# A fused transformer-style block in float32: the first modulation computed by halves of its columns and summed straight into columns, with the first weight unit interleaved between its parts

## Chip, cores and metric

The kernel runs on one core of one Trainium2 chip. The metric is the device time of one execution in microseconds (us); lower is better. The kernel is given as one Python program that writes the instruction stream of each engine: TensorE (PE), VectorE (DVE), ScalarE (ACT), GpSimd (POOL) and SyncE (SP, which issues all DMAs). The engines meet through semaphores alone, and each works off its own list in order.

## What is computed

One layer of a residual block on x of 1 x 1024 x 1024 and a conditioning vector c of 1024. What matters here is its beginning:

```python
c_act = jax.nn.silu(c)
mod = c_act @ w_ada[l] + b_ada[l]                       # 1024 -> 6 x 1024
shift1, scale1, gate1, shift2, scale2, gate2 = jnp.split(mod, N_MOD, axis=-1)
h = _rmsnorm(x, norm_mix_g[l]) * (1.0 + scale1) + shift1
z = h @ w_in[l]                                         # 1024 -> 6144
...
```

After it come the convolution, the gated recurrence, the spatial gating, the branch projections, the output projection, a second modulated norm, the up projection, a convolution and the down projection, and a last norm. All of that is the same in both kernels.

## The kernel before

**Layout.** Activations are kept transposed: channels on the 128 partitions in 8 tiles (KT = 8, KH = 4), tokens along the free dimension (S = 1024 in two halves of 512). A float32 product is made of three products of rounded operands: each operand is split into a high part (made by ACT) and a low part (the difference, made by DVE). The weight's halves are `wop` (four slots, filled by `hi(n)` on ACT, L1109, and `lo(n)` on DVE, L1648); the normed input's halves are `yq` (made by `norm_high` on ACT, L1164, and `norm_low` on DVE, L1715).

**Units.** The input projection runs as units, one after the other on PE. The first, G0, is plain: `first_gates` (L854) takes 12 matmuls for each of the 8 channel tiles, in two groups of 6, and needs `norm_low(k)` of a tile before its 12. From the second, G1, on a unit is done in seven block products (`product7`, L764, 12 matmuls each) in the order b11, t1, t2, b22, t3, b21, t4. t1 to t4 are sums and differences of normed blocks. DVE makes them (`u_sum`, L1719), ACT rounds them (`u_high`, L1179 and L1183) and DVE makes the low parts (`u_low`, L1729 and L1733). POOL makes four sums of weight blocks for each such unit (L617 to L628).

**The beginning.** SP loads x, the parameter rows, the columns of `w_ada` for scale1 (`ada_s`) and shift1 (`ada_h`), 4 MB each, and then weights. PE transposes x (L689), DVE and ACT copy it out of PSUM, and ACT sums squares (L1132). ACT's last steps of this stretch are the copies of the parameter columns (L1124), which PE awaits before it starts the modulation, a table load and the square root (L1151); DVE makes the diagonal matrix of inverse norms (L1697), and PE spreads it over the partitions (L728, the result stays in `ps3`).

**The modulation.** c_act lies as 8 columns, `cact`. For scale1 and shift1 in turn, PE makes rows: `modulation_row` (L708) has a column of `cact` as its weight, 128x1, and streams a row tile of `w_ada` of 1024 columns. This is done for four of the eight tiles; DVE sums the other four, scaled, into an accumulator (`mod_pieces`, L1685 and L1687), and PE adds that up over the partitions (`add_row`, L712). The result is a row of 1024 numbers on one partition. ACT and DVE copy half of it each out of PSUM (L1155, L1703), and PE turns it into columns with eight matmuls whose weight is a 1x128 piece (`row_to_columns`, L717). DVE adds the bias. In float32 each of these matmuls shows as two records in the profile.

**The order of the rest.** `normed(k)` (L1710, DVE) multiplies x by the inverse norm, `scaled(k)` (L1160, ACT) by 1 + scale. When shift is there as columns (`shift_ready`), ACT starts `norm_high(0)`, DVE follows with `norm_low(0)`, and PE starts G0. The place of each piece of work on DVE and ACT is written out by hand (DVE L1736 to L1776, ACT L1186 to L1206). Nothing plans it.

Of the kernel before, what the change touches and what calls it, by code (L numbers as in the profile page):

```python
# [11 lines left out]
P = 128  # L12
# [5 lines left out]
def build(nc, a, out):  # L18
# [54 lines left out]
    with ExitStack() as ctx:  # L73
# [41 lines left out]
        ada_s = place("ada_s", [KT, D], F32, "H")  # L115
        ada_h = place("ada_h", [KT, D], F32, "Y", 2 * QUAD)
# [5 lines left out]
        scale_row = place("scale_row", [D], F32, "WSP", 2 * TILE)  # L122
        shift_row = place("shift_row", [D], F32, "WSP", 3 * TILE)
        scale_acc = place("scale_acc", [D], F32, "WSP", 1 * TILE)
        shift_acc = place("shift_acc", [D], F32, "T", 1 * TILE)
# [105 lines left out]
        def blocks(t):  # L231
# [6 lines left out]
        scale_landed = [sem(f"scale_landed{i}") for i in range(KT // 2)]  # L238
        shift_landed = [sem(f"shift_landed{i}") for i in range(KT // 2)]
# [3 lines left out]
        acc_ready, row_sum, row_ready, row_cols, s1_ready, shift_ready = (  # L243
            sem(x) for x in ("acc_ready", "row_sum", "row_ready", "row_cols", "s1_ready", "shift_ready"))
        xhat_ready, tn_ready, norm_hi, norm_lo, spilled = sem("xhat_ready"), sem("tn_ready"), sem("norm_hi"), sem("norm_lo"), sem("spilled")
# [159 lines left out]
        def _(sp):  # L405
# [11 lines left out]
            def load_modulation(dst, part, landed):  # L417
                for i in range(KT // 2):
                    k = slice(ADA_CHUNKS[i], ADA_CHUNKS[i + 1])
                    sp.dma_start(dst[:, k, :], w_ada[:, k, part * D:(part + 1) * D]).then_inc(landed[i], 16)  # L420
# [237 lines left out]
        def _(pe):  # L658
# [47 lines left out]
            def modulation_row(psum, w, k, first):  # L706
                for h in range(2):
                    nc.tensor.matmul(psum[0:1, h, :], cact[:, k:k + 1], w[:, k, H[h]], start=first, stop=False)  # L708

            def add_row(psum, acc):  # L710
                for h in range(2):
                    last = nc.tensor.matmul(psum[0:1, h, :], ones[:, 0:1], acc[:, H[h]], start=False, stop=True)  # L712
                return last

            def row_to_columns(psum, row):
                for j in range(KT):
                    last = nc.tensor.matmul(psum[:, j:j + 1], row[0:1, j * P:(j + 1) * P], ones[0:1, 0:1], start=True, stop=True)  # L717
                return last
# [3 lines left out]
            for k in SCALE_ROWS:  # L722
                pe.wait_ge(scale_landed[CHUNK_OF[k]], 16)
                modulation_row(ps[1], ada_s, k, k == SCALE_ROWS[0])
                if k == SCALE_ROWS[1]:
                    pe.wait_ge(x_diag, 1)
                    for h in range(2):
                        norm = nc.tensor.matmul(ps[3][:, h, :], ones[:, :],  # L728
                                                diag0[:, HB * h:HB * h + HB, :].rearrange("p b t -> p (b t)"),
                                                start=True, stop=True)  # L730
                    norm.then_inc(x_rbc, 1)
            pe.wait_ge(acc_ready, 1)
            add_row(ps[1], scale_acc).then_inc(row_sum, 1)
            pe.wait_ge(row_ready, 2)
            row_to_columns(ps[0][:, 0, :], scale_row).then_inc(row_cols, 1)
            for k in SHIFT_ROWS:
                pe.wait_ge(shift_landed[CHUNK_OF[k]], 16)
                modulation_row(ps[2], ada_h, k, k == SHIFT_ROWS[0])
            pe.wait_ge(acc_ready, 2)
            add_row(ps[2], shift_acc).then_inc(row_sum, 1)  # L740
            pe.wait_ge(row_ready, 4)
            row_to_columns(ps[0][:, 1, :], shift_row).then_inc(row_cols, 1)
# [102 lines left out]
            def first_gates():  # L845
                for k in range(KT):
                    pe.wait_ge(norm_lo, k + 1)
                    for s, psum in enumerate(BANKS[0]):
                        n = 2 * (k // KH) + s
                        if k % KH == 0:  # L850
                            ready(n)
                        for w, x in PRODUCTS:
                            for h in range(2):
                                done = nc.tensor.matmul(psum[:, h, :], wop[n][:, w, k % KH, :], normed(k, x, h),  # L854
                                                        start=(k == 0 and w == 0 and x == 0), stop=(k == KT - 1 and w == 1))
                        if k % KH == KH - 1:
                            done.then_inc(used, 1)
# [243 lines left out]
        def _(act):  # L1101
# [25 lines left out]
            for c in range(4):  # L1127
                act.wait_ge(x_landed[c], 16)
                for i in (2 * c, 2 * c + 1):
                    if i:  # L1130
                        act.wait_ge(x_squared, i)
                    nc.scalar.activation(sq0[:, :], xtok[:, i, :], ACT.Square, accum_out=ss[:, i:i + 1])\  # L1132
                        .then_inc(x_squared, 1)
                for i in (2 * c, 2 * c + 1):
# [4 lines left out]
                if c == 1:  # L1139
# [5 lines left out]
                    nc.scalar.activation(lt[:, 1, :], lt[:, 0, :], ACT.Exp, scale=-1.0).then_inc(lam_e, 1)  # L1145
            act.wait_ge(param_T, 2)
            for t in range(1, len(ROWS)):
                param_copy(t)
            act.wait_ge(eps_made, 1)
            act.wait_ge(x_squared, NB)  # L1150
            nc.scalar.activation(rs[:, :], ss[:, :], ACT.Sqrt, bias=epsc, scale=1.0 / D).then_inc(x_root, 1)  # L1151

            def row_half(row, psum, n):
                act.wait_ge(row_sum, n)
                nc.scalar.activation(row[0:1, H[0]], psum[0:1, 0, :], ACT.Copy).then_inc(row_ready, 1)  # L1155

            def scaled(k):
                act.wait_ge(s1_ready, 1)
                act.wait_ge(xhat_ready, k + 1)
                nc.scalar.activation(tn[:, k, :], tn[:, k, :], ACT.Identity, scale=s1[:, k:k + 1]).then_inc(tn_ready, 1)  # L1160
# [25 lines left out]
            row_half(scale_row, ps[1], 1)  # L1186
            for k in range(KH):
                scaled(k)
            hi(0)
            scaled(KH)  # L1190
            row_half(shift_row, ps[2], 2)
            hi(1)
            scaled(KH + 1)
# [5 lines left out]
            scaled(KT - 2)  # L1199
            scaled(KT - 1)  # L1200
# [432 lines left out]
        def _(dve):  # L1633
# [29 lines left out]
            def modulation(dst, part, g):  # L1663
                return V.scalar_tensor_tensor(dst[:, :], mod[:, part * KT:(part + 1) * KT], 1.0, C(g, 0, KT),
                                              ALU.add, ALU.mult)
# [4 lines left out]
            V.memset(eps_t[:, :], EPS).then_inc(eps_made, 1)  # L1670
            for i in range(NB):
# [9 lines left out]
            def mod_pieces(acc, w, pieces, k0, landed, done):  # L1681
                for k in pieces:
                    dve.wait_ge(landed[CHUNK_OF[k]], 16)
                    if k == k0:
                        ins = V.tensor_scalar(acc[:, :], w[:, k, :], cact[:, k:k + 1], None, ALU.mult)  # L1685
                    else:
                        ins = V.scalar_tensor_tensor(acc[:, :], w[:, k, :], cact[:, k:k + 1], acc[:, :], ALU.mult, ALU.add)  # L1687
                    if done is not None and k == pieces[-1]:
                        ins.then_inc(done, 1)
                    else:  # L1690
                        step(ins)

            dve.wait_ge(cact_ready, 1)
            mod_pieces(scale_acc, ada_s, (0,), 0, scale_landed, None)
# [4 lines left out]
            mod_pieces(scale_acc, ada_s, (4, 5, 7), 0, scale_landed, acc_ready)  # L1699

            def row_half(row, psum, n):
                dve.wait_ge(row_sum, n)
                V.tensor_copy(row[0:1, H[1]], psum[0:1, 1, :]).then_inc(row_ready, 1)  # L1703

            def normed(k):
# [4 lines left out]
                V.tensor_tensor(tn[:, k, :], x0T[:, k, :], flat(ps[3]), ALU.mult).then_inc(xhat_ready, 1)  # L1710
# [25 lines left out]

            normed(0)
            row_half(scale_row, ps[1], 1)
            normed(1)
            dve.wait_ge(row_cols, 1)  # L1740
            step(V.tensor_tensor(mod[:, KT:2 * KT], ps[0][:, 0, 0:KT], C("b_ada", KT, KT), ALU.add))
            modulation(s1, 1, "norm_mix_g").then_inc(s1_ready, 1)
            normed(2)
            mod_pieces(shift_acc, ada_h, (0, 1), 0, shift_landed, None)
            normed(3)
            mod_pieces(shift_acc, ada_h, (4, 5), 0, shift_landed, acc_ready)
            normed(4)
            lo(0)
            row_half(shift_row, ps[2], 2)
            normed(5)  # L1750
            lo(1)
            dve.wait_ge(row_cols, 2)
            step(V.tensor_tensor(mod[:, 0:KT], ps[0][:, 1, 0:KT], C("b_ada", 0, KT), ALU.add))
# [591 lines left out]
```

## Time and profile before

| | us |
|---|---|
| median of 3 runs (lowest, highest) | 1575.05 (1574.47, 1578.14) |
| the profiled execution | 1574.12 |
| its span, first to last instruction | 1572.1 |
| PE busy | 1536.0 (98%) |
| DVE busy | 1185.2 (75%) |
| ACT busy | 805.2 (51%) |
| POOL busy | 386.2 (25%) |

The span is 2.0 us shorter than the profiled execution's own time. PE busy counts pipelined matmuls by modelled ends, so it can't be read as PE at its peak. The change touches what happens up to about 85 us. The lists of the engines behind that are the same in both kernels.

### The profile page before, as it was taken

How to read it: one execution, taken by the hardware profiler on the slowest of the kernel's cores; microseconds unless marked ns; L12 is line 12 of the kernel's file. 1: busy time of each engine (PE TensorE's matmuls, PEld its weight loads, DVE VectorE, ACT ScalarE, POOL GpSimd, SP SyncE). 2: the span in 40 equal slices, each digit the busy share in tenths (PEclk: the TensorE clock that was granted, in tenths of full speed). 3: DMA queues.
4: the chain of work that ended last, by engine and by line, in shares of the span. 5: the costliest groups of instructions: out<-in, count | busy, mean ns of one | idle time of the engine just before them, and what ended most of it. 6: DMA issues, size and time to landing. Idle time of an engine off the chain costs nothing.

```text
span 1572.1 us, 19429 instructions
## 1 busy us (share of the span) xinstructions
PE 1536.0 (98%) x6860; PEld 1254.4 (80%) x6860; DVE 1185.2 (75%) x1418; ACT 805.2 (51%) x1194; POOL 386.2 (25%) x292
## 2 busy tenths in 40 slices
PE   7999999999999999999998989999999999999998
PEld 3677777888888888888886878888888888888886
DVE  5968889845565685466337999999999987788885
ACT  4648888745545461112123655555555554444446
POOL 0232344332122200000000233333333331233324
PEclk9999999999999999999999999999999999999999
DMA  9331223222322347667210134444444446677722
GB/s 364 133 107 57 82 67 101 65 83 81 101 77 92 107 142 234 180 214 241 94 54 28 49 133 158 151 153 147 148 148 148 150 139 224 208 246 253 253 68 107
DMA packets 197791, 219.55 MB, mean 140 GB/s; under 512 B 8928, under 2 KB 155712, under 8 KB 197056
## 3 DMA queue, kind: packets, MB, share of 16 engines
q1 hardware_dynamic: 197696, 218.32, 41.9%
q8 instruction: 55, 0.90, 0.2%
q14 instruction: 40, 0.33, 0.1%
HBM read 160.61 MB, written 57.67 MB: 139 GB/s over the span
## 4 chain that ended last, share of the span: by engine, by line
PE 82%; DVE 12%; issue 3%; ACT 2%; DMA 0%; POOLq 0%; POOL 0%; ACTq 0%; DVEq 0%
PE ps L764 57%; PE ps L835 15%; DVE wop L1648 3%; DVE xc L1805 2%; PE ps L854 2%; PE ps L958 1%; PE ps L1048 1%; PE ps L708 1%; PE ps L1030 1%; DVE ps L1661 1%; PE ps L901 1%; DVE ti L1823 1%; DVE hidw L2125 1%; ACT wop L1109 1%; DVE m L1828 1%
## 5 line engine op out<-in xcount | busy, mean ns | idle before, releaser
L1648 DVE TENSOR_TENSOR wop<-raw,wop 128x512 fp32r<-128x512 f32 (+1 forms) x523 | 378.8, 731 | 177.2 <-ACT wop L1109 174.9
L1109 ACT ACTIVATE wop<-raw 128x512 fp32r<-128x512 f32 (+1 forms) x523 | 296.5, 569 | 391.1 <-PE ps L764 187.8
L764 PE MATMUL ps<-yq,wop 128*128 128x512 f32 x1716 | 415.9, 392 | 5.9 <-DVE yq L2084 4.7
L764 PEld LDWEIGHTS ps<-yq,wop 128*128 128x128 f32 x1716 | 323.5, 189 | 76.4 <-issue 4.0
L617 POOL TENSOR_TENSOR raw<-raw,raw 128x512 f32<-128x512 f32 (+1 forms) x65 | 96.3, 1482 | 889.2 <-DVE wop L1648 648.6
L764 PE MATMUL ps<-dq,wop 128*128 128x512 f32 x840 | 190.6, 389 | 0.0
L764 PEld LDWEIGHTS ps<-dq,wop 128*128 128x128 f32 x840 | 157.7, 188 | 32.7
L764 PE MATMUL ps<-t4q,wop 128*128 128x512 f32 x540 | 132.9, 396 | 6.8 <-DVE ps L1661 6.8
L764 PE MATMUL ps<-t3q,wop 128*128 128x512 f32 x540 | 130.7, 391 | 2.0 <-issue 1.7
L764 PE MATMUL ps<-t2q,wop 128*128 128x512 f32 x540 | 130.5, 391 | 0.5 <-ACT snap_p L1119 0.5
L764 PE MATMUL ps<-t1q,wop 128*128 128x512 f32 x540 | 130.6, 391 | 0.0
L764 PEld LDWEIGHTS ps<-t4q,wop 128*128 128x128 f32 x540 | 101.6, 190 | 32.3 <-DVE ps L1661 11.4
L1119 ACT ACTIVATE snap_p<-ps 128x512 f32<-128x512 f32 x130 | 77.6, 597 | 93.1 <-PE ps L764 93.0
L2125 DVE SCALAR_TENSOR_TENSOR hidw<-ps,pc,hidw 128x1023 f32<-128x1023 f32 x96 | 122.4, 1276 | 0.9
L1661 DVE TENSOR_TENSOR ps<-ps,snap_p 128x512 f32<-128x512 f32 x130 | 90.2, 694 | 43.1 <-PE ps L764 42.1
L764 PEld LDWEIGHTS ps<-t2q,wop 128*128 128x128 f32 x540 | 101.1, 188 | 22.7 <-ACT snap_p L1119 1.2
L764 PEld LDWEIGHTS ps<-t3q,wop 128*128 128x128 f32 x540 | 100.6, 188 | 23.3 <-issue 2.1
L764 PEld LDWEIGHTS ps<-t1q,wop 128*128 128x128 f32 x540 | 100.8, 188 | 20.6
L628 POOL TENSOR_TENSOR raw<-raw,raw 128x512 f32<-128x512 f32 (+1 forms) x65 | 75.4, 1160 | 89.2 <-DVE wop L1648 85.8
L624 POOL TENSOR_TENSOR raw<-raw,raw 128x512 f32<-128x512 f32 (+1 forms) x65 | 80.9, 1244 | 64.5 <-DVE wop L1648 60.5
L620 POOL TENSOR_TENSOR raw<-raw,raw 128x512 f32<-128x512 f32 (+1 forms) x65 | 90.2, 1387 | 9.3
L835 PE MATMUL ps<-ya_split,wop 128*128 128x512 f32 x384 | 87.8, 390 | 0.0
(235 smaller groups left out, 1929.0 us busy)
## 6 DMA issues: line engine op xcount, KB each, us to landing
dq<-hid_keep SPq DMA_DIRECT2D x35, 1024.0 KB, 7.1
raw<-in_w_in SPq DMA_DIRECT2D x96, 256.0 KB, 3.3
raw<-in_w_up SPq DMA_DIRECT2D x96, 256.0 KB, 3.3
hid_keep<-part_b SPq DMA_DIRECT2D x40, 512.0 KB, 3.0
ada_ring<-in_w_ada SPq DMA_DIRECT2D x32, 512.0 KB, 4.6
hid_keep<-part_t SPq DMA_DIRECT2D x20, 512.0 KB, 2.7
raw<-in_w_down SPq DMA_DIRECT2D x80, 128.0 KB, 2.4
gate_keep<-tg SPq DMA_DIRECT2D x16, 512.0 KB, 4.0
```

What stands on the lines that cost most here:

```text
L617: nc.gpsimd.tensor_tensor(s1, a21, a22, ALU.add).then_inc(s_made, 1)
L620: nc.gpsimd.tensor_tensor(a21, a11, a21, ALU.subtract).then_inc(s_made, 1)
L624: nc.gpsimd.tensor_tensor(a11, s1, a11, ALU.subtract).then_inc(s_made, 1)
L628: nc.gpsimd.tensor_tensor(s1, a12, a11, ALU.subtract).then_inc(s_made, 1)
L764: done = nc.tensor.matmul(bank, left[:, w, lk, :], right[:, x, rk, :], start=(first and w == 0 and x == 0), stop=(last and w == 1), skip_g ...
L835: done = nc.tensor.matmul(psum[:, h, :], wop[n % 4][:, w, k % KH, :], right(k, x, h), start=(k == 0 and w == 0 and x == 0), stop=(k == KT ...
L854: done = nc.tensor.matmul(psum[:, h, :], wop[n][:, w, k % KH, :], normed(k, x, h), start=(k == 0 and w == 0 and x == 0), stop=(k == KT - 1 ...
L1109: nc.scalar.activation(wop[n % 4][:, 0, 0:depth[n], :], raw[slot][:, 0:depth[n], :], ACT.Copy).then_inc(f_hi, 1)
L1119: nc.scalar.activation(dst[:, :], src, ACT.Copy).then_inc(snapped, 1)
L1648: V.tensor_tensor(wop[n % 4][:, 1, 0:kd, :], raw[slot_of[n][0]][:, 0:kd, :], wop[n % 4][:, 0, 0:kd, :].bitcast(F32), ALU.subtract).then_in ...
L1661: V.tensor_tensor(out_b, in_b, kept[:, :], ALU.add).then_inc(joined, 1)
L2125: tap = V.scalar_tensor_tensor(dst[:, d:S], src[:, 0:S - d], C("ffn_conv_w01" if k < 2 else "ffn_conv_w2", k % 2 * 2 * FT + f), dst[:, d:S ...
```

## The change

- `w_ada` is loaded in four parts of 512 columns, `ada_w[0..3]`: scale1 of the channel tiles 0 to 3, shift1 of the same, scale1 of tiles 4 to 7, shift1 of the same. Each is 2 MB, in one DMA of 6 row tiles and one of 2. The weights of G0 are loaded between them: A11 and A21 ahead of part 2, A12 and A22 ahead of part 3.
- For each part PE makes columns at once: the weight is a 128x128 block of `w_ada`, and the moving operand is one column of `cact`. Four matmuls for each row tile, all summed in PSUM (`modulation_columns`). A matmul of the identity with zeros opens the sum (`modulation_begin`), and four matmuls with the accumulator of DVE as their weight close it (`modulation_end`). PE takes 4, 4, 5 and 5 row tiles of the parts, DVE the other 4, 4, 3 and 3, now 512 wide.
- Rows, their copies out of PSUM and `row_to_columns` are gone, and so is `scaled(k)` on ACT: `normed(k)` on DVE now multiplies by scale and inverse norm in one instruction.
- G0 starts when parts 0 and 1 are done. Part 2 is begun just ahead of its tile 0 and ended ahead of tile 1; part 3 is begun ahead of tile 3 and ended ahead of tile 4. `shift_ready` now counts two halves.
- ACT takes the square root ahead of the last copy of x, and loads its table after the fourth square. It copies the last parameter columns behind both.
- DVE's and ACT's lists up to G1 are written in a new order.

```diff
-        ADA_CHUNKS = (0, 3, 6, 7, 8)
-        CHUNK_OF = (0, 0, 0, 1, 1, 1, 2, 3)
-        SCALE_ROWS, SHIFT_ROWS = (1, 2, 3, 6), (2, 3, 6, 7)
+        ADA_SPLIT = 6
+        SCALE_PARTS, SHIFT_PARTS = (0, 2), (1, 3)
+        PE_ROWS = ((0, 1, 2, 6), (0, 1, 2, 6), (0, 1, 2, 3, 6), (0, 1, 2, 3, 6))
...
-            load_modulation(ada_s, 1, scale_landed)
-            load_modulation(ada_h, 0, shift_landed)
-            weights(0)
+            load_modulation(0)
+            load_modulation(1)
+            weights(0, 0, 2)
+            load_modulation(2)
+            weights(0, 2, 4)
+            load_modulation(3)
             weights(1, 0, 2)
...
+            def modulation_columns(p, rows):
+                for k in rows:
+                    pe.wait_ge(ada_landed[p][k // ADA_SPLIT], 16)
+                    for j in range(KH):
+                        nc.tensor.matmul(ps[0][:, p % 2, P + KH * p + j:P + KH * p + j + 1], ada_w[p][:, k, j * P:(j + 1) * P],
+                                         cact[:, k:k + 1], start=False, stop=False, skip_group_check=True)
+
+            def modulation_begin(p):
+                nc.tensor.matmul(ps[0][:, p % 2, P + KH * p:P + KH * p + KH], ident[:, :], dsh[:, :], start=True, stop=False,
+                                 skip_group_check=True)
+                modulation_columns(p, PE_ROWS[p][:-1])
+
+            def modulation_end(p):
+                modulation_columns(p, PE_ROWS[p][-1:])
+                pe.wait_ge(acc_ready, p + 1)
+                for j in range(KH):
+                    last = nc.tensor.matmul(ps[0][:, p % 2, P + KH * p + j:P + KH * p + j + 1], ada_sum1[p % 2][:, j * P:(j + 1) * P],
+                                            ones[:, 0:1], start=False, stop=True, skip_group_check=True)
+                last.then_inc(cols_ready, 1)
...
+            modulation_begin(0)
+            pe.wait_ge(x_diag, 1)
+            for h in range(2):
+                norm = nc.tensor.matmul(ps[3][:, h, :], ones[:, :],
+                                        diag0[:, HB * h:HB * h + HB, :].rearrange("p b t -> p (b t)"),
+                                        start=True, stop=True)
+            norm.then_inc(x_rbc, 1)
+            modulation_end(0)
+            modulation_begin(1)
+            modulation_end(1)
...
             def first_gates():
+                pe.wait_ge(shift_ready, 1)
+                modulation_begin(2)
                 for k in range(KT):
+                    if k == 1:
+                        modulation_end(2)
+                    if k == KH - 1:
+                        modulation_begin(3)
+                    if k == KH:
+                        modulation_end(3)
                     pe.wait_ge(norm_lo, k + 1)
...
-                V.tensor_tensor(tn[:, k, :], x0T[:, k, :], flat(ps[3]), ALU.mult).then_inc(xhat_ready, 1)
+                V.scalar_tensor_tensor(tn[:, k, :], x0T[:, k, :], s1[:, k:k + 1], flat(ps[3]), ALU.mult, ALU.mult).then_inc(tn_ready, 1)
```

The order of PE around the start of G0, before. `ps2` and `ps1` are the outputs of G0, `ps0` holds the columns of the modulation.

```order
L708 MATMUL ps2<-ada_h_73,cact_182 1x512 [waits shift_landed3]
L708 MATMUL ps2<-ada_h_73,cact_182 1x512
L712 MATMUL ps2<-shift_acc_82,ones_177 1x512 [waits acc_ready]
L712 MATMUL ps2<-shift_acc_82,ones_177 1x512
L717 MATMUL ps0<-ones_177,shift_row_80 128x1 [waits row_ready]
L717 MATMUL ps0<-ones_177,shift_row_80 128x1 x7
L854 MATMUL ps2<-yq_49,wop0_63 128x512 [waits f_lo,norm_lo]
L854 MATMUL ps2<-yq_49,wop0_63 128x512 x5
L854 MATMUL ps1<-yq_49,wop1_64 128x512 [waits f_lo]
L854 MATMUL ps1<-yq_49,wop1_64 128x512 x5
```

And after, from the end of tile 2 of G0 to its tile 4:

```order
L857 MATMUL ps1<-yq_49,wop1_64 128x512 x6
L713 MATMUL ps0<-dsh_196,ident_176 128x4
L709 MATMUL ps0<-cact_182,ada_w3_75 128x1 [waits ada_landed3_0]
L709 MATMUL ps0<-cact_182,ada_w3_75 128x1 x3
...
L857 MATMUL ps2<-yq_49,wop0_63 128x512 [waits norm_lo]
L857 MATMUL ps2<-yq_49,wop0_63 128x512 x5
L857 MATMUL ps1<-yq_49,wop1_64 128x512 x6
L709 MATMUL ps0<-cact_182,ada_w3_75 128x1 [waits ada_landed3_1]
L709 MATMUL ps0<-cact_182,ada_w3_75 128x1 x3
L721 MATMUL ps0<-ones_177,ada_sum1_1_82 128x1 [waits acc_ready]
L721 MATMUL ps0<-ones_177,ada_sum1_1_82 128x1 x3
L857 MATMUL ps2<-yq_49,wop2_65 128x512 [waits f_lo,norm_lo]
```

The shift of the upper tiles, which was complete ahead of G0, is now complete between its tiles 3 and 4.

DVE at the same place, before, from the low parts of tiles 2 and 3 on:

```order
L1715 SCALAR_TENSOR_TENSOR yq<-tn,mod,yq 128x2x512 x2
L1719 TENSOR_TENSOR t1w<-tn 128x2048
L1648 TENSOR_TENSOR wop_65<-raw_59,wop_65 128x512
L1648 TENSOR_TENSOR wop_66<-raw_60,wop_66 128x512
L1715 SCALAR_TENSOR_TENSOR yq<-tn,mod,yq 128x2x512 x4
L1648 TENSOR_TENSOR wop_63<-raw_61,wop_63 128x512
L1719 TENSOR_TENSOR t2w<-tn,t1w 128x2048
L1729 TENSOR_TENSOR t1q<-t1w,t1q 128x2048
L1719 TENSOR_TENSOR tn<-tn,t2w 128x4x512
L1648 TENSOR_TENSOR wop_64<-raw_59,wop_64 128x512
```

And after, from the wait for the last columns (`cols_ready`) on:

```order
L1687 TENSOR_TENSOR mod_178<-ps0,pc_175 128x4 [waits cols_ready]
L1757 TENSOR_TENSOR dsh1_195<-mod_178 128x4 [waits shift_ready]
L1710 SCALAR_TENSOR_TENSOR yq_49<-tn_77,mod_178,yq_49 128x2x512 [waits norm_hi]
L1705 SCALAR_TENSOR_TENSOR tn_77<-x0T_76,s1_179,ps3 128x1024
L1710 SCALAR_TENSOR_TENSOR yq_49<-tn_77,mod_178,yq_49 128x2x512 [waits norm_hi]
L1714 TENSOR_TENSOR t1w_54<-tn_77 128x2048
L1710 SCALAR_TENSOR_TENSOR yq_49<-tn_77,mod_178,yq_49 128x2x512 [waits norm_hi]
L1714 TENSOR_TENSOR t2w_55<-tn_77,t1w_54 128x2048 [waits u_made]
L1710 SCALAR_TENSOR_TENSOR yq_49<-tn_77,mod_178,yq_49 128x2x512 [waits norm_hi]
L1637 TENSOR_TENSOR wop0_63<-raw4_61,wop0_63 128x512 [waits f_hi]
L1637 TENSOR_TENSOR wop1_64<-raw2_59,wop1_64 128x512 [waits f_hi]
```

The low parts of tiles 4 to 7, one `normed` and both sums of the t chain now stand behind a wait for PE's columns.

## Rows read from the trace of the kernel before

**Rows 1.** Busy time by stage: stretch, length, busy time and instructions, PEclk, DMA share, GB/s

```profile
17.60:19.94 2.34, 0.00 (x0) 0.00 (x1) 1.43 (x2) 2.32 (x7) 0.00 (x0) 1.00 1.04 415
19.94:51.14 31.20, 26.64 (x77) 8.10 (x77) 21.46 (x26) 12.95 (x15) 0.00 (x0) 0.85 1.05 392
51.14:75.06 23.92, 23.92 (x97) 19.62 (x98) 23.82 (x16) 15.80 (x19) 7.03 (x3) 0.92 0.07 21
```

**Rows 2.** PE in order of time up to G0: start, length, what, idle before

```profile
19.94 5.29 PE L708 MATMUL ps<-ada_s,cact 128*1 128x512 f32 x8 [2.34 <-ACT pc L1124]
25.16 1.98 PE L728 MATMUL ps<-diag,ones 128*128 128x512 f32 x4
33.16 2.23 PE L717 MATMUL ps<-ones,scale_row 1*128 1x1 f32 x16 [0.77 <-DVE scale_row L1703]
46.19 1.94 PE L717 MATMUL ps<-ones,shift_row 1*128 1x1 f32 x16 [0.77 <-DVE shift_row L1703]
51.14 1.22 PE L854 MATMUL ps<-yq,wop 128*128 128x512 f32 x2 [3.01 <-DVE yq L1715]
```

**Rows 3.** DVE in order of time: first modulation piece, then from the first low part on

```profile
19.41 0.75 DVE L1685 TENSOR_SCALAR scale_acc<-ada_s,cact 128x1024 f32<-128x1024 f32 x1 [0.91 <-DMA ada_s<-in_w_ada]
...
49.80 1.28 DVE L1715 SCALAR_TENSOR_TENSOR yq<-tn,mod,yq 128x1024 fp32r<-128x1024 f32 x1 [1.27 <-ACT yq L1164]
51.00 1.21 DVE L1710 TENSOR_TENSOR tn<-x0T,ps 128x1024 f32<-128x1024 f32 x1
56.85 2.28 DVE L1719 TENSOR_TENSOR t1w<-tn 128x2048 f32<-128x2048 f32 x1
60.26 6.93 DVE L1715 SCALAR_TENSOR_TENSOR yq<-tn,mod,yq 128x1024 fp32r<-128x1024 f32 x4
70.10 3.20 DVE L1729 TENSOR_TENSOR t1q<-t1w,t1q 128x2048 fp32r<-128x2048 f32 x1
76.03 3.77 DVE L1733 SCALAR_TENSOR_TENSOR t2q<-t2w,mod,t2q 128x512 fp32r<-128x512 f32 x4
79.72 0.68 DVE L1648 TENSOR_TENSOR wop<-raw,wop 128x512 fp32r<-128x512 f32 x1
80.32 2.28 DVE L1719 TENSOR_TENSOR tn<-tn 128x2048 f32<-128x2048 f32 x1
85.23 2.74 DVE L1733 SCALAR_TENSOR_TENSOR t3q<-tn,dsh,t3q 128x512 fp32r<-128x512 f32 x4 [1.43 <-ACT t3q L1183]
```

**Rows 4.** PE in units G1 and R0: product t3, and two products in a row

```profile
88.07 3.00 PE L764 MATMUL ps<-t3q,wop 128*128 128x512 f32 x12 [1.72 <-issue]
...
99.34 2.88 PE L764 MATMUL ps<-t1q,wop 128*128 128x512 f32 x12
102.06 2.88 PE L764 MATMUL ps<-t2q,wop 128*128 128x512 f32 x12
```

**Rows 5.** ACT in order of time, from the fourth square to the root

```profile
18.50 1.00 ACT L1137 ACTIVATE x0T<-ps 128x1024 f32<-128x1024 f32 x1
19.41 0.48 ACT L1124 ACTIVATE pc<-ps 128x96 f32<-128x96 f32 x3
19.91 1.28 ACT L1151 ACT_TABLE_LOAD   x1
21.20 0.30 ACT L1151 ACTIVATE rs<-ss,eps_t 128x8 f32<-128x8 f32 x1
```

**Rows 6.** PE at 623 us: column sums with 128x128 weights, and what follows

```profile
623.81 1.84 PE L703 MATMUL ps<-ones,ada_acc 128*128 128x1 f32 x16
625.51 3.25 PE L835 MATMUL ps<-ya_split,wop 128*128 128x512 f32 x13
```

**Rows 7.** PE by stretch: length, PE busy and matmuls, PEclk, DMA share, GB/s

```profile
34.65:38.07 3.42, 3.42 (x9) 0.50 1.16 304
48.30:55.14 6.84, 4.00 (x9) 0.50 0.44 144
85.80:89.20 3.40, 1.68 (x8) 1.00 0.54 189
```

More of the change, by code:

```diff
@@ L121, in build @@
         diag0 = place("diag0", [NB, P], F32, "T", 3 * TILE)
[L122 to L125, printed above, removed]
+        ada_sum1 = [place(f"ada_sum1_{i}", [HALF], F32, "T", 1 * TILE + i * 4 * HALF) for i in range(2)]
         xc_split = place("xc_split", [2, S], F32R, "X")
@@ L415, in load_x, with load_modulation @@
                 sp.dma_start(xtok[:, 2 * i:2 * i + 2, :], x_tok[:, 2 * i:2 * i + 2, :]).then_inc(x_landed[i], 16)
[L417 to L420, printed above, removed]
+            def load_modulation(p):
+                c0 = (D if p in SCALE_PARTS else 0) + p // 2 * HALF
+                for i, k in enumerate((slice(0, ADA_SPLIT), slice(ADA_SPLIT, KT))):
+                    sp.dma_start(ada_w[p][:, k, :], w_ada[:, k, c0:c0 + HALF]).then_inc(ada_landed[p][i], 16)
             def weights(pos, start=0, stop=4):
@@ L704, in column_sums @@
                 return last
[L706 to L718, printed above, removed]
+            def modulation_columns(p, rows):
[4 more added lines that the diff above has]
+                                         cact[:, k:k + 1], start=False, stop=False, skip_group_check=True)
@@ L720, in _ @@
             for e in range(2):
                 pe.wait_ge(xT_copied[e], COPIER.count(e))
[L722 to L731, printed above, removed]
@@ L1133, in _ @@
                         .then_inc(x_squared, 1)
+                if c == 3:
+                    act.wait_ge(x_squared, NB)
+                    nc.scalar.activation(rs[:, :], ss[:, :], ACT.Sqrt, bias=epsc, scale=1.0 / D).then_inc(x_root, 1)
                 for i in (2 * c, 2 * c + 1):
@@ L1148, in _ @@
                 param_copy(t)
[L1149 to L1160, printed above, removed]
             def norm_high(k):
@@ L1198, in _ @@
             hi(3)
[L1199 to L1200 removed]
+            act.wait_ge(shift_ready, 2)
             for k in range(KH, KT):
@@ L1680, in _, with mod_pieces, mod_columns, scale_columns @@
                     V.tensor_tensor(lt[:, 0, :], lt[:, 2, :], lam, ALU.max).then_inc(lam_e, 1)
[L1681 to L1685, printed above, removed]
-                    else:
-                        ins = V.scalar_tensor_tensor(acc[:, :], w[:, k, :], cact[:, k:k + 1], acc[:, :], ALU.mult, ALU.add)
-                    if done is not None and k == pieces[-1]:
-                        ins.then_inc(done, 1)
+            def mod_pieces(p, rows):
+                acc, mine = ada_sum1[p % 2], [k for k in range(KT) if k not in PE_ROWS[p]]
+                for k in rows:
+                    dve.wait_ge(ada_landed[p][k // ADA_SPLIT], 16)
+                    if k == mine[0]:
+                        ins = V.tensor_scalar(acc[:, :], ada_w[p][:, k, :], cact[:, k:k + 1], None, ALU.mult)
+                    else:
+                        ins = V.scalar_tensor_tensor(acc[:, :], ada_w[p][:, k, :], cact[:, k:k + 1], acc[:, :], ALU.mult, ALU.add)
+                    if k == mine[-1]:
+                        ins.then_inc(acc_ready, 1)
                     else:
                         step(ins)
+            def mod_columns(p):
+                dve.wait_ge(cols_ready, p + 1)
+                c0 = (KT if p in SCALE_PARTS else 0) + p // 2 * KH
+                return V.tensor_tensor(mod[:, c0:c0 + KH], ps[0][:, p % 2, P + KH * p:P + KH * p + KH], C("b_ada", c0, KH), ALU.add)
+            def scale_columns(p):
+                step(mod_columns(p))
+                step(modulation(s1, 1, "norm_mix_g", p // 2 * KH, p // 2 * KH + KH))
             dve.wait_ge(cact_ready, 1)
-            mod_pieces(scale_acc, ada_s, (0,), 0, scale_landed, None)
             dve.wait_ge(x_root, 1)
```

93 lines of the change are left out of this document (38 added, 55 removed).

## The prediction, made before any run of the changed kernel

> **What bounds the kernel now.** I read the busy time by stage first. From the start of the modulation at 19.94 to G0's first matmul at 51.14 PE is busy for 26.6 of 31.2 us, DVE for only 21.5 of them; from there to G0's end at 75.06 PE is without a gap and DVE is busy for 23.8 of 23.9 [rows 1]. So PE carries the first stretch, and both are full in the second. PE's list in order of time shows what the first stretch is made of: row matmuls, the spreading of the norms, eight column matmuls each for scale and shift, two waits of 0.77 for the copies of a row out of PSUM, and 3.01 us of waiting for the first low part [rows 2].
>
> Then I followed G1, since it shows who is late behind G0. Its product t3 starts at 88.07 after 1.72 us of idling that is put down to issue [rows 4]. DVE's list names the cause. The last sum, which t3 is made from, runs from 80.32 to 82.60, ACT rounds it, and DVE's low part of t3 ends at 87.97 [rows 3]. **So the end of this beginning is set by DVE**, which works almost without a pause from 49.80 to 82.60. PE could be at t3 1.7 us sooner and gain nothing. Behind t3 the lists are equal and all of it shifts with t3's start. The question is therefore: does t3 start ahead of 88.07?
>
> **The change, part by part.**
>
> *ACT's head.* PE awaits the last parameter copies, which end at 19.89. Now the table load (1.28), an added small root and the real root (0.30 each) stand ahead of them [rows 5]: 1.9 us, with the steps between 2.1. PE starts the modulation at about 22.0 instead of 19.94. DVE has the root a microsecond earlier, which nobody needs.
>
> *PE's new work.* A float32 matmul gives two records. Parts 0 and 1 have 2 + 5 x 8 = 42 records each, parts 2 and 3 have 2 + 6 x 8 = 50, together 184. The nearest row is the column sum at 623 us, the same 128x128 weights and one column: 16 records from 623.81 to 625.51, so 0.106 each, 19.5 us in all [rows 6]. The other end is the present column matmul with 1x128 weights, 2.23 / 16 = 0.139 [rows 2]; I take 0.106 for the shape. Before, 48 row and sum records and 32 column records made up most of 26.6 us, so PE's work is hardly less, and 100 of the 184 records now stand behind the start of G0's stretch. To them come the norms, 1.9 [rows 2], and G0's tiles 0 to 3 at 2.72 each, the pace of two products in a row [rows 4], 10.9.
>
> *The clock.* PE ran its first row matmuls partly at 1.2 GHz (mean grant 0.85 in the stretch [rows 1]). After a longer idle time now I count the 26 records ahead of the norms at half speed, +2.8.
>
> *Waits.* 0.3 for the half shift ahead of part 2, 0.5 for DVE's accumulator of part 2. Columns of part 3 are complete at 22.0 + 19.5 + 1.9 + 10.9 + 2.8 + 0.8 = **57.9**.
>
> *DVE behind it.* Its list has everything up to `wop3` done by about 53, so it waits there for some 5 us. Then comes the bias, ACT's first high part, and the low part of tile 4 starts 1.5 later, at 59.4 (before, the same hop put tile 0's at 49.80 [rows 3]). From there to the end of the last sum: four low parts and one `normed` at 1.20 (spacing of two starts), three sums and the low part of t1 at 2.2, three weight low parts at 0.6, t2's low parts 2.7, the last sum 2.3: 21.6. POOL's sums slow DVE: t1's low part took 3.20 against 2.28 for a sum of that size, t2's 3.77 against 2.74 for t3's [rows 3]; +1.9. End at 59.4 + 23.5 = **82.9, against 82.60 before**. The 1.8 us that POOL cost in the four low parts (6.93 against 5.1) are saved, since POOL's first two sums now fall into DVE's wait; this is inside the sum. The 88.07 becomes 88.4.
>
> The page GPSIMD Engine Reference of the Trainium skill, in its table of properties, says that POOL shares its SBUF interfaces with VectorE and contends with instructions of two SBUF inputs. By that rule one more sum would be slowed by about 0.9 us, to 1576.3; the trace shows such a sum beside POOL unslowed, and the measurement decides.
>
> *Costs of nothing.* G0 itself ends at about 73 instead of 75.06: tile 7's low part is ready at 69.9, then 2.7. It is swallowed: product t2 waits for its low parts until 80.7, and t3 waits for the chain above. ACT loses eight `scaled` (9 us), but is not late anywhere. `normed` with its third operand is taken at 1.20 like a low part. The loads: the first 1.5 MB of `w_ada` had landed by 19.41 [rows 3]; at 0.39 MB per us [rows 1] part 1 is complete at 26, needed at 31, part 3 at 39, needed at 50. Loads in pieces of half the length could be a third slower and still be hidden; if this cover were gone, each late microsecond of part 1 or 3 would count fully.
>
> Sum: +0.3. The profiled execution, 1574.12, becomes 1574.4. That run lies 0.9 below the median, so the median of 1575.05 becomes **1575.4**. A difference under 0.3% (4.7 us) can't be told from none here.
>
> **The rivals.**
>
> *Slower: the clock stays at 1.2 GHz over the one-column matmuls.* For: the clock was granted at 0.50 from 34.65, behind 1.5 us of column matmuls and a gap of 0.77, and from 48.30, again right behind them [rows 2, 7]. Within wide products an idle time of 1.72 us left it at 1.00 [rows 7]. So narrow work seems to hold the clock badly, and now it is all that PE does from 22 to 39 but for two matmul pairs. Against: those weights had one row, they came with a gap, and the clock came back at 38.07 over a stretch that began with them. It decides at about 28 to 31 us: if the grant is still 0.50 there, 58 records of parts 0 and 1 and 34 of part 2 cost 0.106 more each (9.8), the norms 1.9, and the first wide matmuls, as from 51.14 on, about 1.5. That is 13, and up to 17 if part 3 loses the clock again. All of it lies ahead of 57.9, so it counts in full: about 1588, between 1583 and 1592. If it comes back after the norms, it costs 2, and that belongs to the forecast.
>
> The Trainium skill (TensorE: Matmul & The Clock Gate, section What's actually happening) has the clock set by how busy PE has been. By that rule unbroken narrow work is busy work and the forecast stands at 1575.4; it does not say whether matmuls of one column count, and only the rows above bear on that.
>
> *Slower by price:* a record costs 0.139. 158 of them at full clock: +5.2, 1580.6.
>
> *Faster:* DVE's wait for part 3 is the slack. If the clock is full from the start (-2.8), POOL costs DVE nothing behind 59.4 (-1.9) and the waits of 0.8 are gone, t3 starts 5.5 sooner, 1569.9. Each alone stays within 0.3%. That the change does what it says isn't in doubt: both orders show it.
>
> **How the numbers follow.** Forecast with its neighbours (1571 to 1579): 0.45. Clock: 0.32. Price or another late piece: 0.06. Faster: 0.17. So same 0.45, slower 0.38, faster 0.17. The range leaves out a part of the faster case and the tail of the clock's: 1569.5 to 1589.
>
> **What would show it.** Right: part 3's columns at 57 to 59 us, DVE idle 4 to 6 us ahead of them, G0 done near 73, t3 of G1 at 88 to 89 after a wait of over 2 us, records of one column 0.10 to 0.11 apart, grant at 1.00 by 28 to 31. Wrong: a grant of 0.50 past 31; one-column records apart by more than 0.12 at full clock; a t3 that does not wait for DVE; or any wait for a load.

## The result, and the profile after

The changed kernel takes **1589.49 us** (median of 4 runs, 1587.38 to 1591.42), the kernel before in the same comparison 1574.76 (4 runs, 1574.07 to 1578.14). The ratio is 1.01, with a 95% interval of 1.0088 to 1.0113: slower by 14.7 us. The forecast was 1575.4 with a range up to 1589.0. The rival "the clock stays at 1.2 GHz" gave about 1588, between 1583 and 1592. The profiled spans, 1589.1 against 1572.1, lie 17.0 apart, more than the medians: the change's profile is of one of its longer executions.

PE in order of time, the part that answers to [rows 2] (start, length, what, idle before):

```profile
22.37 0.59 PE L713 MATMUL ps<-dsh,ident 128*128 128x4 f32 x2 [4.54 <-ACT pc L1127]
22.82 5.26 PE L709 MATMUL ps<-cact,ada_w 128*128 128x1 f32 x24
27.94 3.76 PE L731 MATMUL ps<-diag,ones 128*128 128x512 f32 x4
...
33.62 5.44 PE L709 MATMUL ps<-cact,ada_w 128*128 128x1 f32 x32
...
41.47 6.96 PE L709 MATMUL ps<-cact,ada_w 128*128 128x1 f32 x32
48.30 4.89 PE L857 MATMUL ps<-yq,wop 128*128 128x512 f32 x12
53.02 0.95 PE L709 MATMUL ps<-cact,ada_w 128*128 128x1 f32 x8
53.83 1.03 PE L721 MATMUL ps<-ones,ada_sum 128*128 128x1 f32 x8
54.72 5.69 PE L857 MATMUL ps<-yq,wop 128*128 128x512 f32 x24
60.39 4.95 PE L709 MATMUL ps<-cact,ada_w 128*128 128x1 f32 x32
65.20 4.97 PE L857 MATMUL ps<-yq,wop 128*128 128x512 f32 x12
```

Equal work stands here at two prices. Eight column records at 53.02 are 0.10 apart, the eight behind them 0.11; the 32 at 41.47 are 0.21 apart. A tile of G0 (x12) takes 4.89 at 48.30, while two tiles (x24) take 5.69 at 54.72. The stretches of the same profile say which clock was granted (length, PE, PEld, DVE, ACT, POOL, PEclk, DMA share, GB/s), and answer to [rows 1, 7]:

```profile
22.00:28.00 6.00, 5.63 (x27) 5.63 (x27) 5.15 (x8) 0.80 (x4) 0.00 (x0) 0.50 1.09 357
...
31.95:35.35 3.40, 3.40 (x32) 3.40 (x32) 1.64 (x4) 0.00 (x0) 0.00 (x0) 0.99 1.12 339
35.35:48.00 12.65, 12.40 (x59) 12.31 (x58) 8.98 (x11) 5.42 (x6) 0.00 (x0) 0.50 1.11 433
...
52.20:62.20 10.00, 10.00 (x63) 8.85 (x61) 7.10 (x10) 0.00 (x0) 0.58 (x1) 0.99 0.09 26
62.20:69.20 7.00, 7.00 (x28) 6.13 (x28) 0.00 (x0) 0.00 (x0) 2.34 (x2) 0.53 0.13 37
```

The clock came back at about 32 us, behind the norms, and was gone again from 35.35 on. At that moment PE stood in the middle of part 1's 32 records, without a pause before it. From 62.2 it fell once more, inside part 3's 32 records. PE is busy for 12.40 of 12.65 us at a grant of 0.50: being busy in this sense did not hold the clock.

DVE and PE behind part 3, which answer to [rows 3, 4]:

```profile
71.89 0.16 DVE L1687 TENSOR_TENSOR mod<-ps,pc 128x4 f32<-128x4 f32 x1 [9.75 <-PE ps L721]
73.26 1.28 DVE L1710 SCALAR_TENSOR_TENSOR yq<-tn,mod,yq 128x1024 fp32r<-128x1024 f32 x1 [1.02 <-ACT yq L1160]
...
87.05 2.29 DVE L1714 TENSOR_TENSOR tn<-tn,t2w 128x2048 f32<-128x2048 f32 x1
91.19 1.31 DVE L1637 TENSOR_TENSOR wop<-raw,wop 128x512 fp32r<-128x512 f32 x1 [1.84 <-ACT wop L1112]
```
```profile
102.82 3.00 PE L759 MATMUL ps<-t3q,wop 128*128 128x512 f32 x12 [1.72 <-issue]
```

DVE waits 9.75 us for the columns of part 3, which come at 71.89. Product t3 of G1 starts at 102.82 instead of 88.07, 14.75 later. Nothing absorbs it: at about 584 us the first matmuls of a group (L830) and at 1334 those of another (L1033) are still 14.7 and 14.6 us late. The other 2.4 us between the two spans arise behind 1340 us, where the lists are the same; no run isolates what they are. So 14.75 at t3 and 14.7 between the medians agree only roughly.

### The profile page after: what moved, and what is told of

Same layout as the page of the kernel before. It is cut to its first block, busy times and chain, and to the rows that moved or that the text cites. A ratio compares the mean times of both kernels' runs of the same rounds, so it can differ in the third digit from the quotient of the medians.

```text
span 1589.1 us, 19648 instructions
## 1 busy us (share of the span) xinstructions
PE 1548.6 (97%) x6972; PEld 1280.8 (81%) x6972; DVE 1181.9 (74%) x1426; ACT 795.1 (50%) x1185; POOL 387.7 (24%) x292
## 4 chain that ended last, share of the span: by engine, by line
PE 80%; DVE 12%; issue 3%; ACT 3%; POOL 1%; DMA 1%; POOLq 0%; ACTq 0%; DVEq 0%
PE ps L759 55%; PE ps L830 15%; DVE wop L1637 3%; DVE xc L1801 2%; PE ps L709 2%; PE ps L961 1%; PE ps L1051 1%; PE ps L1033 1%; DVE ps L1650 1%; PE ps L857 1%; PE ps L904 1%; DVE ti L1819 1%; DVE hidw L2121 1%; ACT wop L1112 1%; DVE m L1824 1%
## 5 line engine op out<-in xcount | busy, mean ns | idle before, releaser
L830 PE MATMUL ps<-yb_split,wop 128*128 128x512 f32 x384 | 87.8, 390 | 0.0
```

The costliest lines, as they stand in the source:

```text
L830: done = nc.tensor.matmul(psum[:, h, :], wop[n % 4][:, w, k % KH, :], right(k, x, h), start=(k == 0 and w == 0 and x == 0), stop=(k == KT ...
```

## Experiments

Each run compares with the kernel before on the same chip. The median of the kernel before was 1574.3 beside the first four (wide64, wide128, insert1, insert64), 1573.8 beside the next four (wide16, head64, early64, both64) and 1573.3 beside the last three.

**wide64: the same matmuls, but 64 equal columns wide.** The weights, the records and their order are those of the change. Only the moving operand is wider, the sums lie at other PSUM columns to make room, and DVE reads one column in 64.

```diff
-                        nc.tensor.matmul(ps[0][:, p % 2, P + KH * p + j:P + KH * p + j + 1], ada_w[p][:, k, j * P:(j + 1) * P],
-                                         cact[:, k:k + 1], start=False, stop=False, skip_group_check=True)
+                        nc.tensor.matmul(ps[0][:, p % 2, part_at(p) + WIDE * j:part_at(p) + WIDE * j + WIDE], ada_w[p][:, k, j * P:(j + 1) * P],
+                                         cact[:, k:k + 1].to_broadcast([P, WIDE]), start=False, stop=False, skip_group_check=True)
```

(The zero matmul of `modulation_begin` and the sum in `modulation_end` are widened in the same way.)

> The changed kernel, but every one-column matmul of the modulation now moves 64 equal columns (the same column of cact, or of ones, 64 times) and DVE reads one in 64 of the results; same weights, same order, same number of matmuls. Clock theory (one-column matmuls do not hold TensorE's clock, and the half clock is the whole loss): the grant returns to 1.00 before the norms, stays there through parts 1, 2 and 3, the columns of part 3 are complete at 57 to 60 us instead of 71.8, G1's t3 starts at 88 to 90 instead of 102.8, total 1574 to 1578. Price theory (the loss lies in the number of weight loads and their order on TensorE, whatever the clock): the wider operand cannot help, 1589 or more. Third (waiting on VectorE's list sets the time): under 2 us change, 1588 to 1590.

Measured: 1579.64 (5 runs, 1577.35 to 1580.99), ratio 1.0037 (1.0022 to 1.0051). By the medians 9.4 of 14.7 us are back. PE, DVE, then the stretches:

```profile
36.97 3.68 PE L714 MATMUL ps<-cact,ada_w 128*128 128x64 f32 x32
40.46 3.00 PE L862 MATMUL ps<-yq,wop 128*128 128x512 f32 x12
...
90.49 3.00 PE L764 MATMUL ps<-t3q,wop 128*128 128x512 f32 x12 [0.23 <-issue]
```
```profile
59.55 0.16 DVE L1692 TENSOR_TENSOR mod<-ps,pc 128x4 f32<-128x4 f32 x1 [5.69 <-PE ps L726]
```
```profile
22.00:28.00 6.00, 6.00 (x25) 4.68 (x25) 4.02 (x6) 0.42 (x1) 0.00 (x0) 0.57 1.09 361
...
36.00:52.00 16.00, 15.65 (x97) 13.81 (x97) 15.58 (x20) 5.42 (x6) 0.00 (x0) 1.00 1.04 402
```

The 32 records of part 2 take 3.68 instead of 6.96, although they stream 64 times as much. Part 3's columns come at 59.55 instead of 71.89. The clock theory had the direction and most of the size, but claimed too much: the grant was 0.50 until about 28.5 us, over the norms too, t3 came at 90.49 instead of 88 to 90, and the median is 1579.64 instead of 1574 to 1578. So the half clock is not the whole loss. The profile is of the fastest of the five executions.

**wide128 and wide16: how wide it has to be.** `WIDE` is 128 or 16, with the sums placed in PSUM to fit.

> The same with 128 equal columns. Clock theory: clock as with 64, but 128 columns no longer hide behind the weight load, so up to 0.05 us more for each of 184 records (+0 to +9 us against 64 columns). Price theory: 1589 plus those 0 to 9 us.

> The change with each one-column modulation matmul moving 16 equal columns instead (DVE reads one in 16). Between 1 column (clock at 0.50 for 10.3 + 17 us in this stretch, 1589.5) and 64 columns (0.50 only until 28.5, 1579.6). Theory (it is the idle array, few moved columns per weight load, that lets the clock fall): with 16 columns the clock still falls somewhere in parts 0 to 2, since the array is busy for a quarter as long as with 64; time between 1582 and 1589. Rival (any more than a single column will do, one column being a special form of matmul): the clock stays as in wide64, time 1578 to 1581.

Measured, one run each: 1578.73 with 128 columns, 1586.41 with 16. With 128 the clock is at 1.00 from 28 us to 60 and 32 records take 3.73, so 128 columns cost no more than 64, against the expectation's up to 0.05 for each record. With 16 it fell as in the change, for part 2 too, but the 32 records of part 3, from 59.26 to 62.80, kept 1.00:

```profile
34.00:50.00 16.00, 15.74 (x68) 15.12 (x68) 12.02 (x14) 5.41 (x6) 0.00 (x0) 0.50 1.06 408
...
60.00:64.00 4.00, 4.00 (x32) 3.83 (x32) 0.93 (x2) 0.00 (x0) 2.91 (x2) 1.00 0.23 66
```

So the loss is no property of the single column alone: 16 lose the clock too, though not in every part; 64 and 128, once the clock was up, did not lose it in any part.

**insert1 and insert64: the same in isolation.** The kernel before, with 48 unneeded matmuls (96 records) in the fourth ZV unit, where the clock is at 1.00 and PE has no idle time. One column in the first, 64 in the second:

```diff
+                if SEQ[pos] == ("ZV", 3) and w == 4:
+                    pe.wait_ge(*outputs_read(pos - 1, 0))
+                    for j in range(48):
+                        nc.tensor.matmul(past[0][:, 0, 0:1], ident[:, :], ones[:, 0:1], start=True, stop=True)
```

> The kernel before, with 48 unneeded float32 matmuls (128x128 weights, ONE column moved; 96 records) put in one row into the densest stretch, in the fourth ZV unit near 350 us. Nothing waits for them and TensorE has no idle time there. Clock theory: the grant falls to 0.50 inside the row though TensorE never pauses, so the row takes 14 to 20 us instead of the 10.2 that 96 records of 0.106 take, and the first wide matmuls behind it run at half speed; total +15 to +21. Rival (the clock fell only because of pauses and the late start of the beginning): the grant stays at 1.00, total +10 to +11.

> The same inserted row, but each matmul moves 64 columns. Clock theory: the grant stays at 1.00, row 10 to 12 us, total +10 to +12. If the number of weight loads without much streaming is what lowers the clock, it falls here too: +15 to +21.

Measured, one run each: 1594.02 and 1586.14. PE and stretches of the one with one column:

```profile
347.66 17.21 PE L891 MATMUL ps<-ones,ident 128*128 128x1 f32 x96
364.73 4.66 PE L764 MATMUL ps<-t3q,wop 128*128 128x512 f32 x12
```
```profile
345.00:351.00 6.00, 6.00 (x44) 5.53 (x42) 2.72 (x3) 1.75 (x3) 3.18 (x3) 1.00 0.15 44
...
352.00:358.00 6.00, 6.00 (x30) 6.00 (x29) 0.00 (x0) 0.00 (x0) 0.00 (x0) 0.50 0.00 0
```

And of the one with 64:

```profile
349.15 10.82 PE L891 MATMUL ps<-ones,ident 128*128 128x64 f32 x96
359.78 3.01 PE L764 MATMUL ps<-t3q,wop 128*128 128x512 f32 x12
```
```profile
352.00:358.00 6.00, 6.00 (x56) 6.00 (x56) 0.00 (x0) 0.00 (x0) 0.10 (x1) 1.00 0.01 3
```

PE never pauses in either. With one column it runs 30 records in 6 us at 0.50, with 64 it runs 56 at 1.00. The price is 17.21 against 10.82 for the row, and the product behind it takes 4.66 instead of 3.01. Both hit their expectations: +19.7 and +11.8 against the kernel before. Hardly a load is under way when the clock falls in insert1 (DMA share 0.01 from 350 to 351 us, 0.06 in the next), and insert64 has more (0.29 from 351 to 352) and keeps 1.00. This shows it apart from the rest of the change: the clock falls by the kind of work, with no gap to blame.

**head64, early64, both64: what is left of the loss.** On the 64-column version, ACT's head is put back as before (`head64`), part 3 is begun ahead of G0's tile 1 and ended ahead of tile 2 (`early64`), or both.

```diff
-                if c == 3:
-                    act.wait_ge(x_squared, NB)
-                    nc.scalar.activation(rs[:, :], ss[:, :], ACT.Sqrt, bias=epsc, scale=1.0 / D).then_inc(x_root, 1)
...
-                    act.wait_ge(eps_made, 1)
-                    nc.scalar.activation(sd[:, :], epsc, ACT.Sqrt)
...
             for t in range(1, len(ROWS)):
                 param_copy(t)
+            act.wait_ge(eps_made, 1)
+            act.wait_ge(x_squared, NB)
+            nc.scalar.activation(rs[:, :], ss[:, :], ACT.Sqrt, bias=epsc, scale=1.0 / D).then_inc(x_root, 1)
```
```diff
-                    if k == KH - 1:
+                    if k == 1:
                         modulation_begin(3)
-                    if k == KH:
+                    if k == 2:
                         modulation_end(3)
```

> The 64-column version of the change, with ACT's list as in the kernel before at its head: the parameter copies stand ahead of the small root and the real root, so that PE can start the modulation about 2 us sooner (20.0 instead of 21.1 to 22.4 us). Theory (the clock is no longer lost, and what is left of the loss is the chain head, part 3, DVE): part 3's columns and DVE's low part of tile 4 come about as much sooner as PE starts, t3 of G1 starts 1 to 2.5 us ahead of the 90.49 us of wide64 (88 to 89.5), time 1575 to 1578.5 against a kernel before of 1574.3 and wide64's 1579.6. Rival (DVE's list behind part 3 is held by POOL and ACT, not by part 3): t3 stays at 90.2 or later and the time at 1579 to 1580. Second rival (the clock falls at the start whatever is done, and longer after an earlier start): half speed until 28 us or more, which gives less than 1 us.

> The 64-column version of the change, with part 3 begun ahead of G0's tile 1 and ended ahead of tile 2 (instead of tiles 3 and 4). G0's tiles lie 2.7 us apart, so part 3's columns should be complete about 5.5 us sooner (54 instead of 59.6 us), if DVE's accumulator of part 3 is done by then (DVE's idle time ahead of part 3's columns was 5.69 us in wide64). Theory (DVE's wait for part 3 is what the chain to t3 passes through): DVE's idle time ahead of part 3's columns falls to under 2.5 us, t3 of G1 starts at 85 to 88 instead of 90.49, time 1572 to 1575. Rival (the list order costs nothing, since DVE is busy anyway and its idle time only moves, for example to the POOL sum that its later weight low part waits for): t3 stays at 89.5 to 90.5 and the time within 1 us of wide64's 1579.6.

> Both edits together on the 64-column version: ACT's head as before, and part 3 begun ahead of G0's tile 1 and ended ahead of tile 2. Theory (both are pieces of one chain): DVE hardly idle ahead of part 3's columns, t3 of G1 at 83 to 86.5 against 88.07 in the kernel before, time 1569.5 to 1573, that is ahead of both kernels. Rival (the chain to t3 passes into DVE's own work and POOL's sums as soon as part 3 is early): no more than the better of the two single edits, t3 at 87 to 88, time 1573 to 1575. Part 0's clock: half speed to about 28 us in both cases.

Measured, 10 runs each: head64 1577.83 (ratio 1.0024, 1.0012 to 1.0035; its interval overlaps wide64's), early64 1574.60 (1.0008, 0.9999 to 1.0017), both64 1571.80 (0.9985, 0.9974 to 0.9995). From early64 to both64, the same edit of ACT's head, the intervals don't overlap: 2.8 us. early64, both64 and the median of head64 came as the theory had them. Part 3's columns in early64 and both64:

```profile
56.05 0.16 DVE L1692 TENSOR_TENSOR mod<-ps,pc 128x4 f32<-128x4 f32 x1 [0.23 <-PE ps L726]
```
```profile
54.09 0.16 DVE L1690 TENSOR_TENSOR mod<-ps,pc 128x4 f32<-128x4 f32 x1 [0.22 <-PE ps L726]
```

DVE's wait of 5.69 us in wide64 has shrunk to 0.2, and t3 starts at 87.78 and 85.25. head64's profile missed its expectation for t3 (86.22 instead of 88 to 89.5): in that execution the clock was at 1.00 from 20 to 30 us, in both64's, with the same list up to there, at 0.50. The ten times of head64 run from 1573.24 to 1579.95, and its profiled execution (1574.18) is one of the lower. So what happens at the start differs from one execution to the next, and only medians compare. Nor is t3 the whole of the time: the profiled both64 reaches it 2.8 us ahead of the kernel before and ends 1.0 ahead.

**both1b: the order edits without the wide operand.** The change as it is, with the two edits of both64.

> The change with its one-column matmuls as they are, but with the two order edits of both64 (ACT's head as before; part 3 begun ahead of G0's tile 1 and ended ahead of tile 2). Theory (the low clock is a loss of its own of about 10 us at t3, and the order edits take away the rest): time 1580 to 1585, t3 of G1 at 93 to 99, the clock still at 0.50 for most of 22 to 32 and 35 to 52 us. Rival (with part 3 early the chain has slack enough to hide the low clock): 1574 to 1578. Second rival (the order edits only help once the clock is high): 1588 to 1590, as the change itself.

Measured: 1584.04 (4 runs, 1582.62 to 1587.93), ratio 1.0060 (1.0044 to 1.0076); t3 at 98.54 in the profile, which is of the longest of the four. The theory had 1580 to 1585 and 93 to 99. Stretches and the DVE row of part 3:

```profile
20.65:48.00 27.35, 27.10 (x116) 24.95 (x115) 16.60 (x23) 7.47 (x10) 0.00 (x0) 0.50 1.09 391
48.00:60.00 12.00, 12.00 (x60) 11.16 (x60) 8.73 (x12) 0.00 (x0) 0.00 (x0) 0.64 0.39 141
```
```profile
67.59 0.16 DVE L1685 TENSOR_TENSOR mod<-ps,pc 128x4 f32<-128x4 f32 x1 [5.95 <-PE ps L721]
```

By the ratios the order edits bring some 6 us here (1.0100 to 1.0060) and 8 from wide64 to both64 (1.0037 to 0.9985); the wide operand brings 10 without them and 12 with them. The low clock is a loss of its own.

**swap64b and fill64b: two more edits on both64.** `swap64b` puts t2's low parts ahead of DVE's weight low part that had waited 1.9 us for ACT. `fill64b` is swap64b with seven unneeded matmuls in PE's idle time ahead of part 0.

```diff
-            lo(6)
             u_low(1)
+            lo(6)
```
```diff
+            for _ in range(7):
+                nc.tensor.matmul(ps[0][:, 0, 256:384], ident[:, :], ident[:, :], start=True, stop=True, skip_group_check=True)
             pe.wait_ge(param_col, len(ROWS))
```

> both64 with one more edit: on DVE, t2's four low parts stand ahead of the weight low part that waited 1.9 us for ACT's rounding, which itself waits for a POOL sum. Theory (that POOL sum is slow beside DVE's two-input sums, and through ACT it holds DVE's list ahead of the last sum): the wait disappears ahead of the last sum, t3 of G1 starts 1.5 to 2 us sooner (83.2 to 83.8 instead of 85.2), time 1.5 to 2 us below both64: 1569.5 to 1570.5 on the same footing of the kernel before (1573.8). Rival (t2's low parts wait as long for ACT's high parts, or the wait moves ahead of t3's low parts): t3 stays at 84.9 or later and the time within 0.5 us of both64's 1571.8.

> The kernel of swap64b with seven unneeded fp32 matmuls (128x128, 128 columns) on PE in its idle time of 1.3 to 1.8 us ahead of part 0, written to PSUM columns that part 2 overwrites later. In the profile of both64 the granted clock was 0.50 from 19.9 to 30 us, behind that idle time; in that of head64, with the same list up to there, it was 1.00. Theory (the idle time brings the clock down in some executions and not in others, and that costs up to 4 us at t3): with the idle time filled the clock is 1.00 from 20 to 30 us, the median 1.5 to 3.5 us below swap64b's, and the spread of the runs smaller. Rival (the fall comes from what PE did earlier, from 10 to 17 us, with its waits for the loads of x): the same distribution as swap64b, median within 0.7 us.

Measured, 12 runs each: 1571.78 (ratio 0.9988, 0.9978 to 0.9999) and 1570.58 (0.9983, 0.9973 to 0.9992). The swap gained nothing that can be measured over both64 (0.9985). PE and DVE in swap64b:

```profile
74.96 4.46 PE L764 MATMUL ps<-t2q,wop 128*128 128x512 f32 x12 [2.88 <-DVE wop L1640]
...
82.49 3.00 PE L764 MATMUL ps<-t3q,wop 128*128 128x512 f32 x12 [0.34 <-issue]
```
```profile
54.55 3.38 DVE L1717 TENSOR_TENSOR t1w<-tn 128x2048 f32<-128x2048 f32 x1
...
64.69 3.37 DVE L1727 TENSOR_TENSOR t1q<-t1w,t1q 128x2048 fp32r<-128x2048 f32 x1
67.99 3.37 DVE L1717 TENSOR_TENSOR tn<-tn,t2w 128x2048 f32<-128x2048 f32 x1
```

The weight part that was put back is one that product t2 needs. The wait moved from DVE to PE, and the product behind it took 4.46, in part at a grant of 0.50. That does not settle why the medians are equal, for DVE lost time as well: three of its operations of 2048 columns took 3.4 each, beside sums of POOL, where both64 had 2.3, and t3 came 32.9 us behind part 3's columns (82.49 against 49.58) instead of 31.2. The two profiles also began at different clocks, 1.00 here and 0.50 in both64, so what the swap does by itself at t3 isn't shown. The rival had the time right; its t3 of 84.9 or later did not come, and its reason is not shown. fill64b is inconclusive: its median is 1.2 us below swap64b's, between what the theory and the rival gave, the intervals overlap, the spread of the times is no smaller (1568.63 to 1575.33 against 1569.08 to 1575.44), and the clock stood at 1.00 from 20 to 30 us in both profiles. It is the fastest version that was run, 0.17% below the kernel before.

## Why the prediction was wrong

**The step that failed** is the clock: "I count the 26 records ahead of the norms at half speed, +2.8", and with it the choice of "if it comes back after the norms, it costs 2, and that belongs to the forecast". The clock did come back behind the norms, and then fell again under the one-column matmuls. In my own steps, the extra over the forecast until the columns of part 3: the norms, from 27.94 to 31.50, 3.6 instead of 1.9; part 1 from 33.40 to 40.76, 7.4 instead of 42 x 0.106 = 4.5; part 2's beginning from 41.02 to 48.30, 7.3 instead of 3.6; tile 0 4.7 instead of 2.72; part 3's beginning 4.9 instead of 3.6; tile 3 4.8 instead of 2.72. Together 1.7 + 2.9 + 3.7 + 2.0 + 1.3 + 2.1 = 13.7 us, against a shift of part 3's columns of 71.89 - 57.9 = 14.0. The rival priced 13, and up to 17 if part 3 loses the clock again. Part 3 did lose it (3.4 of the 13.7), while part of parts 0 and 1 ran at full clock: 16 records behind the norms and the first of part 1. The two offset each other in part, so it is partly luck that the rival's 1588 came so near to 1589.49.

What made me choose wrongly: I weighed "those weights had one row, they came with a gap" as reasons against [rows 2, 7]. Both were beside the point, and insert1 has neither. I also let the unbroken occupation of PE speak for the clock. The Trainium skill (TensorE: Matmul & The Clock Gate, section What's actually happening) has the clock set by how busy PE has been. Read with the profile's busy time, the trace disagrees: with PE busy for 6.00 of 6.00 us the grant was 0.50 with one moved column and 1.00 with 64.

The clock is not all that the forecast had wrong. wide64, with the grant near 1.00 from 28.5 us on, is still 5.3 us above the kernel before by the median, where the forecast had +0.3. Its profile shows part of that: the norms took 3.73, part 3's columns came at 59.55 instead of 57.9, and t3 at 90.49 instead of 88.4. That is the fastest of its executions; what makes the others up to 3.6 us longer no profile shows.

**What held.**
- ACT's head: PE at 22.37, forecast 22.0. By the medians it costs 1.8 us between wide64 and head64 and 2.8 between early64 and both64.
- The price of a record: 0.11 at full clock (forecast 0.106), 0.21 at half. The Trainium skill (TensorE: Matmul & The Clock Gate, section LDWEIGHTS) gives the time of a weight load in ns as its columns divided by 1.2. Worked out for 128 columns that is an estimate of 107 ns, and the trace agrees at full clock.
- DVE behind part 3: from the columns to t3 30.9 us in the change and 30.9 in wide64, forecast 30.5. In both64 it was 31.2, in both1b 31.0, in early64 31.7. **t3 comes 30.9 to 31.7 us after part 3's columns in all versions with this DVE list**, which is the forecast's claim that DVE sets this end. With the swapped list it was 32.9, in swap64b and in fill64b.
- The step after: of 14.75 us at t3 14.6 were still there at 1334 us, nothing absorbed it.
- No load was late in the change: none of PE's waits from part 0 on was for a DMA.

**What was off without changing the outcome.** POOL's contention was taken as +1.9 on DVE's low parts of t1 and t2. They ran in 2.29 and 2.73, unslowed, and POOL's sum took the delay; DVE then paid by waiting 1.84 for ACT. Size right, kind wrong. And the forecast had the place of part 3 as a given: early64 shows that this place in PE's list alone was worth 5 us, which no step of mine asked about.

## What to carry to other kernels

In this kernel a long row of matmuls that each load 128x128 weights and move only a few columns lowered TensorE's clock though PE never paused, and the wide matmuls behind it paid as well. A short row did not: the 16 records at 623 us in the kernel before [rows 6] ran 0.106 apart. Widening the moving operand to 64 equal columns added nothing that could be measured to a record and kept the clock where it was high; it needs only PSUM space and a strided read. When the work of two engines meets at one late event (here part 3's columns), follow the distance from it to the end, see in each version whether it holds (31 us here, but 33 once DVE's list was changed), and ask what may come earlier in the list of the engine that makes it.

## What the runs showed of the hardware that was not expected

- At one and at 16 moved columns per weight load the granted clock fell to 0.50 without a pause (with 16, not in part 3), at 64 and 128 it stayed at 1.00 or came back to it. In insert1 it was 0.50 from 352 us to the row's end and until 368 us, over most of the product behind it.
- A float32 record with 128x128 weights takes 0.11 us at a grant of 1.00 whether it moves 1, 64 or 128 columns (8 records from 53.83 to 54.72 with one; 32 records: 3.68 at 64, 3.73 at 128).
- POOL's 128x512 sum of two operands took 1.27 us while DVE waited, and 6.08 beside DVE's sums of two operands in SBUF, which ran unslowed. POOL in the changed kernel:

```profile
63.41 1.27 POOL L619 TENSOR_TENSOR raw<-raw,raw 128x512 f32<-128x512 f32 x1
84.42 6.08 POOL L623 TENSOR_TENSOR raw<-raw,raw 128x512 f32<-128x512 f32 x1 [19.74 <-DVE wop L1637]
```

  The page GPSIMD Engine Reference of the Trainium skill says, in its table of properties, that the two share SBUF interfaces. The trace agrees, but here the side that lost was POOL. In [rows 3] DVE was slowed too (3.20 against 2.28), and in swap64b again (3.4 against 2.3). Which of them pays when was not tried.
- The same list ran its start at 1.00 in one execution and at 0.50 in another (head64 and both64 from 20 to 30 us). PE had been idle just before for 1.33 us in head64, 1.77 in both64, and 1.61 in swap64b, where the grant was 1.00. What decides it stays open.
